# Feed-forward products from x without its root, padded chunk tiles and another order of filling, in a two-block float32 transformer kernel

## The chip, the cores and the metric

One NeuronCore of a Trainium2 chip runs the whole program in one launch. The metric is the device time in microseconds (us). Times of the kernel before are given as the median of three runs; the trace comes from one more, profiled execution.

## The reference, cut to what matters

Two transformer blocks of width D = 1024 over 256 tokens, in float32. The first block has a gated-delta-rule mixer (8 heads, chunks of 64 tokens) and one feed-forward part; the second has two layers, a gated linear attention (4 heads, chunks of 64) and a latent attention (8 heads), each with a feed-forward part. So there are three feed-forward parts, each behind a norm:

```python
def rmsnorm(t, g):                       # norm over the 1024 channels of a token
    return t * lax.rsqrt(jnp.mean(t * t, -1, keepdims=True) + EPS) * g
h = rmsnorm(x, g) * (1.0 + scale) + shift          # scale, shift: one value for a channel
gu = h @ w_ffn_in                                  # 1024 -> 2 * 2816
x = x + gate * ((silu(gu[..., :2816]) * gu[..., 2816:]) @ w_ffn_out)
# chunk step of the gated delta rule (gated linear attention has the same k_c, v form)
v_new = u_c - w_c @ state
o = q_c @ state + qk_c @ v_new
state = state * exp(gl) + k_c.T @ v_new            # k_c, v_new: 64 tokens of one chunk
```

scale, shift and gate come from products of a conditioning vector ("ada" units in the kernel).

## The kernel before, in words

All data is kept transposed: a tile has 128 channels on the partitions and the T = 256 tokens along the row; KB = 8 such tiles make x (`xT`). Each big product is made exact to float32 from fast products: a weight block of 1024 x 128 is loaded by SyncE (SP) into `w_raw` (4 slots), ScalarE copies it rounded into `w_high` (`high`, L1340 to L1345), VectorE subtracts to get `w_low` (`low`, L1845 to L1850), and the activations have the same two parts. `split_product` (L738) then issues for each of the 8 blocks k of channels three matmuls of 128x128 weights on 256 columns: high by high (L749), high by low (L750), low by high (L751); 24 matmuls make one product of 128 output channels. Everything of an engine is in one queue, and semaphores order the engines; the order of the work is written out by hand.

A feed-forward part (`ffn`, once on each engine: L753 TensorE, L1539 ScalarE, L2250 VectorE) has an up stage of 11 iterations with 4 products each (gate, up, gate, up: two pairs) and a down stage of 4 iterations with 8 pieces each. It is used for n = 1, 4 and 6. Before its first product the norm must be whole:

- VectorE adds the last output block to `xT` and squares each block into `sq` (`add_blocks`, L2156; `add_pairs`, L2202). TensorE sums the squares over partitions (`norm_sum`, L727, matmuls at L734, for blocks 6 and 7 behind the last output product).
- ScalarE makes the root: `norm` (L1319) with Ln (L1325) and Exp (L1327) gives `rstd`.
- VectorE multiplies each block by `nscale` and `rstd` (L2254), ScalarE adds shift and rounds into `h_parts` (L1549), VectorE makes the low part (`h_low`, L1861, at L1865). The first product waits for each of the 8 blocks in turn.

In the up stage ScalarE copies each product out of its PSUM bank (`bank[j % 2]`, L1337), the gates with Silu; VectorE multiplies the pair (L2273), ScalarE rounds it (L1569) and VectorE makes the low part (L2284). In iterations with an ada unit VectorE also does two multiply-adds of 512 columns for each pair (L1827).

The mixer output ahead of n = 4 and 6 comes from `out_part` (L803): plain float32 matmuls (each two records at L811) with weights in slots of `ring`, in the order of j = 0 to 7. `Stream` objects say which slots a weight stream uses: `st_o2` the slots [3, 7, 11, 16, 17, 0, 1, 2], `st_o3` the slots 4 to 11. Ring slots 0 to 3 are the memory of `w_raw`, 4 to 7 of `w_high`, 8 to 11 of `w_low`; 12 to 15 are the memory of `h1_parts`. `st_h2`, the stream of the four gated-linear-attention heads, uses splits in slots 0 to 2 only. SP issues all loads in program order, each after a wait until its slot is free.

In the delta-rule head (`head1`, L876) the step over the four chunks does `kdec[r, t, :]` by `vnew[r, t, :]` (L977) with 64 rows of partitions, r being the chunk's half of a 128-token tile; in the linear attention (`head2`, L1049) it is `kd_tok` by `v_tok` (L1094, L1104). Between such small products TensorE works off a share of the next head's split products (`products`). In the last head (`head2(H2, False, True)`) the shares are output parts instead, and the first waits for the third head's result (`head2_out`, L1066), made by VectorE at L2418.

## Time and profile before

| | us |
|---|---|
| median of three runs | 1410.51 |
| lowest and highest of them | 1408.54, 1417.34 |
| the profiled execution's own time | 1407.37 |
| its span, first to last instruction | 1405.7 |
| mean granted TensorE clock over the span | 0.978 of full speed |

The own time is 1.7 us longer than the span; what lies around the span is not touched by the change. PE is TensorE's matmuls, PEld its weight loads, DVE VectorE, ACT ScalarE, SP the queue that issues DMAs. A matmul's end is modelled in the records, so the distance from one start to the next is what to read, not its duration. A float32 matmul that is not split shows as two records.

### The profile page before, as it was taken

How to read it: one execution, taken by the hardware profiler on the slowest of the kernel's cores; microseconds unless marked ns; L12 is line 12 of the kernel's file. 1: busy time of each engine (PE TensorE's matmuls, PEld its weight loads, DVE VectorE, ACT ScalarE, POOL GpSimd, SP SyncE). 2: the span in 40 equal slices, each digit the busy share in tenths (PEclk: the TensorE clock that was granted, in tenths of full speed). 3: DMA queues.
4: the chain of work that ended last, by engine and by line, in shares of the span. 5: the costliest groups of instructions: out<-in, count | busy, mean ns of one | idle time of the engine just before them, and what ended most of it. 6: DMA issues, size and time to landing. Idle time of an engine off the chain costs nothing.

```text
span 1405.7 us, 26728 instructions
## 1 busy us (share of the span) xinstructions
PE 1324.8 (94%) x9961; PEld 1230.1 (88%) x9961; DVE 927.6 (66%) x1669; ACT 662.8 (47%) x1182; POOL 14.9 (1%) x82
## 2 busy tenths in 40 slices
PE   6899999999999899999899987999999998999997
PEld 3889899998899899999678876999997787999996
DVE  0678888788867678778655644787785542865553
ACT  2555555555555455454554423554542442545542
POOL 4000000000000000000000000000000000000000
PEclk9999999999999999999999998999999999999999
DMA  9656446555354489889668712889797383666562
GB/s 317 196 157 178 137 134 195 165 165 172 114 165 144 133 241 274 265 247 316 173 212 258 225 46 75 240 268 274 215 321 236 107 209 104 189 203 185 159 183 85
DMA packets 400017, 269.96 MB, mean 192 GB/s; under 512 B 9914, under 2 KB 357424, under 8 KB 399936
## 3 DMA queue, kind: packets, MB, share of 16 engines
q1 hardware_dynamic: 399936, 268.83, 64.2%
q8 instruction: 57, 0.93, 0.3%
q14 instruction: 24, 0.20, 0.0%
HBM read 267.75 MB, written 1.05 MB: 191 GB/s over the span
## 4 chain that ended last, share of the span: by engine, by line
PE 82%; DVE 8%; ACT 4%; issue 2%; DMA 2%; SPq 2%; DVEq 0%; ACTq 0%
PE bank L749 20%; PE bank L751 20%; PE bank L750 20%; PE bank L811 4%; DVE w_low L1849 1%; PE bank L1150 1%; PE bank L734 1%; ACT w_high L1345 1%; PE bank L941 1%; PE bank L949 1%; PE bank L950 1%; DMA ring<-in_mla_w_q_up 1%; DVE h_parts L1865 1%; SPq L534 1%; SPq L472 1%
## 5 line engine op out<-in xcount | busy, mean ns | idle before, releaser
L749 PE MATMUL bank<-h_parts,w_high 128*128 128x256 f32 x2016 | 605.0, 300 | 21.1 <-DVE h_parts L1865 16.2
L751 PE MATMUL bank<-h_parts,w_low 128*128 128x256 f32 x2016 | 576.4, 286 | 0.0
L750 PE MATMUL bank<-h_parts,w_high 128*128 128x256 f32 x1952 | 558.7, 286 | 0.0
L1849 DVE TENSOR_TENSOR w_low<-w_raw,w_high 128x1024 fp32r<-128x1024 f32 (+2 forms) x348 | 391.0, 1130 | 101.3 <-ACT w_high L1345 87.4
L749 PEld LDWEIGHTS bank<-h_parts,w_high 128*128 128x128 f32 x2016 | 391.8, 194 | 42.8 <-issue 25.3
L751 PEld LDWEIGHTS bank<-h_parts,w_low 128*128 128x128 f32 x2016 | 392.4, 195 | 0.0
L750 PEld LDWEIGHTS bank<-h_parts,w_high 128*128 128x128 f32 x1952 | 381.3, 195 | 1.3 <-issue 1.0
L1345 ACT ACTIVATE w_high<-w_raw 128x1024 fp32r<-128x1024 f32 (+2 forms) x348 | 338.1, 979 | 78.0 <-PE bank L751 28.5
L749 PE MATMUL bank<-act_parts,w_high 128*128 128x256 f32 x528 | 148.8, 282 | 0.0
L1337 ACT ACTIVATE evac<-bank 128x256 f32<-128x256 f32 x140 | 53.6, 383 | 200.5 <-PE bank L751 199.7
L750 PE MATMUL bank<-act_parts,w_high 128*128 128x256 f32 x528 | 147.4, 279 | 0.0
L751 PE MATMUL bank<-act_parts,w_low 128*128 128x256 f32 x528 | 147.4, 279 | 0.0
L749 PEld LDWEIGHTS bank<-act_parts,w_high 128*128 128x128 f32 x528 | 99.2, 188 | 1.8 <-DVE w_low L1849 1.7
L751 PEld LDWEIGHTS bank<-act_parts,w_low 128*128 128x128 f32 x528 | 99.5, 188 | 0.0
L750 PEld LDWEIGHTS bank<-act_parts,w_high 128*128 128x128 f32 x528 | 99.0, 188 | 0.1
L1827 DVE SCALAR_TENSOR_TENSOR big<-ada_w,cact,big 128x512 f32<-128x512 f32 (+1 forms) x98 | 73.3, 748 | 1.1
L811 PE MATMUL bank<-big,ring 128*128 128x256 f32 x256 | 63.1, 399 | 8.4 <-DVE big L2418 6.6
L811 PEld LDWEIGHTS bank<-big,ring 128*128 128x128 f32 x256 | 49.8, 200 | 16.5 <-DVE big L2418 7.4
L1479 ACT ACTIVATE scratch<-bank 128x256 f32<-128x256 f32 x40 | 15.4, 386 | 88.8 <-PE bank L941 88.7
L2273 DVE TENSOR_TENSOR evac<-evac 128x256 f32<-128x256 f32 x66 | 28.1, 425 | 35.1 <-ACT evac L1337 35.0
L1337 ACT ACTIVATE scratch<-bank 128x256 f32<-128x256 f32 x64 | 24.5, 383 | 54.7 <-PE bank L751 54.5
L2070 DVE TENSOR_TENSOR scratch<-scratch,bank 128x512 f32<-128x512 f32 (+1 forms) x40 | 25.4, 635 | 37.1 <-PE bank L950 37.1
(371 smaller groups left out, 1480.4 us busy)
## 6 DMA issues: line engine op xcount, KB each, us to landing
ada_w<-in_ada_w SPq DMA_DIRECT2D x48, 1024.0 KB, 6.1
w_raw<-in_ffn_w_in SPq DMA_DIRECT2D x88, 512.0 KB, 4.2
w_raw<-in_w_in SPq DMA_DIRECT2D x72, 512.0 KB, 3.8
w_raw<-in_w_ffn_in SPq DMA_DIRECT2D x44, 512.0 KB, 3.9
ada_w<-in_w_ada SPq DMA_DIRECT2D x16, 1024.0 KB, 7.3
w_raw<-in_gla_w_in SPq DMA_DIRECT2D x24, 512.0 KB, 6.2
w_raw<-in_ffn_w_out SPq DMA_DIRECT2D x32, 384.0 KB, 4.3
w_raw<-in_ffn_w_out SPq DMA_DIRECT2D x32, 320.0 KB, 3.4
```

What stands on the lines that cost most here:

```text
L472: sp.dma_start(dst, src(i, j)).then_inc(S(f"landed{s}"), 16)
L749: pe.matmul(acc[:, 0:T], hi[:, n, :], x_high[:, k, :], start=k == 0, stop=False)
L750: pe.matmul(acc[:, 0:T], hi[:, n, :], x_low[:, k, :], start=False, stop=False)
L751: mm = pe.matmul(acc[:, 0:T], lo[:, n, :], x_high[:, k, :], start=False, stop=k == kb - 1)
L811: mm = pe.matmul(accs[j // 2][:, j % 2 * T:(j % 2 + 1) * T], slot(st.slots[j])[:, k, :], rhs[:, k, :], start=k == 0 and j % 2 == 0, stop=k ...
L1337: return act.activation(dst, bank[(j % nacc)][:, 0:T], func, scale=scale).then_inc(S("evacuated"), 1)
L1345: act.activation(w_high[:, s, 0:m], w_raw[:, s, 0:m], ACT.Copy).then_inc(S("rounded"), 1)
L1479: act.activation(xs.rearrange("p a b -> p (a b)"), bank[3][:, 0:NT * P], ACT.Copy).then_inc(S("xs"), 1)
L1827: dve.scalar_tensor_tensor(acc, w, c, acc, ALU.mult, ALU.add).then_inc(S("ada_mac"), 1)
L1849: dve.tensor_tensor(w_low[:, s, 0:m], w_raw[:, s, 0:m], w_high[:, s, 0:m].bitcast(F32), ALU.subtract)\
L2070: dve.tensor_tensor(flat, flat, bank[4][:, 2 * P * part_of.start:], ALU.subtract).then_inc(S("inv"), 1)
L2273: dve.tensor_tensor(prod, prod, evac[:, 2 * q + 1, :], ALU.mult).then_inc(S("ffn_act"), 1)
```

## The change

Four things change.

1. The feed-forward parts take `xs_parts` in place of `h_parts`: x times `nscale`, without the root, in high and low parts, and as two more columns (TW = T + 2 = 258) the shift in high and low parts. Each block is made as soon as it is added: ScalarE copies it with scale (`x_high`) and also squares it, VectorE makes the low part (`x_low`), inside the loops that add the output blocks. A product thus gives W(x * nscale) in 256 columns and W(shift) in the two others. VectorE multiplies a pair's two products by `rstd_wide` (the root, and 1 in the two more columns) straight from two PSUM banks, ScalarE does Silu with column 256 as bias, VectorE adds the other's column 256 and multiplies. The first product of a part runs before its norm is whole; the last squares are summed behind it.
2. `pairs` of PSUM banks: the up stage uses banks 2, 3 and then 0, 1, the down stage 2 and 3.
3. `kdec`, `vnew` and `kd_tok` are padded with zeros, so that L977, L1094 and L1104 use all 128 rows of partitions. GpSimd clears `kdec` and `vnew` at the start; ScalarE writes 3 half tiles of `kdec` where it wrote 2 whole, and 3 of `kd_tok` where it wrote 1.
4. Filling: pieces 0 and 1 of a part's weights are split before it begins; `st_o2` uses the slots [2, 6, 10, 3, 7, 11, 16, 17] and `st_o3` [6, 7, 10, 11, 16, 17, 2, 3]; the output parts of the last linear-attention head take heads 0 and 1 for j = 0 to 5 first, then head 2.

```diff
+        TW = T + 2
+        h1_parts = x_space[:, 0:2 * KB * T].rearrange("p (k a t) -> p k a t", k=KB, a=2)
+        xs_parts = x_space.rearrange("p (k a t) -> p k a t", k=KB, a=2)
-        kdec = piece((NT, P))
+        kdec = piece((NCH, P))
-        kd_tok = piece((NT, P))
+        kd_tok = piece((NCH - 1, P))
-        st_o2 = Stream(1, KB, [3, 7, 11, 16, 17, 0, 1, 2])
+        st_o2 = Stream(1, KB, [2, 6, 10, 3, 7, 11, 16, 17])
-        st_o3 = Stream(1, KB, SplitStream.SLOTS)
+        st_o3 = Stream(1, KB, [6, 7, 10, 11, 16, 17, 2, 3])
+        HIDDEN = pairs[::-1]
+        DOWN = bank[2:4]
-            pool.memset(wz, 0.0).then_inc(S("padded"), 1)
+            for dst in (wz, kdec, vnew):
+                pool.memset(dst, 0.0).then_inc(S("padded"), 1)
...
# TensorE: split_product takes x_high.shape[-1] columns; ffn:
                     for j in range(4):
-                        pe.wait_ge(S("evacuated"), st_f.done(i, j) + 3 - 2)
-                        split_product(st_f, i, j, bank[j % 2], h_parts, ...)
+                        if j % 2 == 0:
+                            pe.wait_ge(S("evacuated"), st_f.done(i, j + 1) + 3 - 4)
+                        elif first:
+                            pe.wait_ge(S("evacuated"), st_f.block0 + 3)
+                        if first and j == 0:
+                            pe.wait_ge(S("shift_low"), m + 1)
+                        split_product(st_f, i, j, HIDDEN[j // 2][:, j % 2, :], xs_parts, ...)
+                        if first and j == 0:
+                            norm_sum(n, range(KB - 2 if n == 1 else 3, KB))
...
-                        pe.matmul(bank[4][:, 0:P], kdec[r, t, :], vnew[r, t, :], start=True, stop=True).then_inc(S("s_done"), 1)
+                        pe.matmul(bank[4][:, 0:P], kdec[:, c, :], vnew[:, t, :], start=True, stop=True).then_inc(S("s_done"), 1)
...
                             if at[0] == 0:
+                                pe.wait_ge(S("head2_out"), H2 - 2)
+                                pe.wait_ge(S("evacuated"), st_h2.end + 3)
+                            if at[0] == 6 * (KB - 2 * DV2):
                                 pe.wait_ge(S("head2_out"), H2 - 1)
-                                pe.wait_ge(S("evacuated"), st_h2.end + 3)
...
             for j in range(KB):
-                if j >= 6:
-                    norm_sum(4, range(3 * (j - 6), 3 * (j - 5)))
+                if j == 6:
+                    norm_sum(4, range(3))
                 for k in range(KB - DV2, KB):
                     out_part(st_o2, OUT2, j, k, big)
-            norm_sum(4, range(KB - 2, KB))
...
# ScalarE
+            def x_high(n, f, shift_sec):
+                act.wait_ge(S("o_added"), 4 + FFN_OF[n] * KB + f + 1)
+                if f == 0:
...
+                    act.activation(xs_parts[:, :, 0, T:TW], shift.broadcast_to([P, KB, TW - T]), ACT.Copy).then_inc(S("shift_high"), 1)
+                act.activation(xs_parts[:, f, 0, 0:T], xT[:, f, :], ACT.Copy, scale=nscale[:, f:f + 1]).then_inc(S("h_ready"), 1)
+                act.activation(sq[:, f, :], xT[:, f, :], ACT.Square).then_inc(S("norm_sq"), 1)
...
             def ffn(n, st_f, st_d, shift_sec):
-                act.wait_ge(S("gemm_done"), st_f.block0)
-                high(st_f, 0, 0, IN_PARTS)
+                high(st_f, 0, 2, IN_PARTS, free=st_f.block0)
                 norm(n)
-                for f in range(KB):
...
+                        gate = evac_wide[:, 2 * q, :]
+                        act.wait_ge(S("evacuated"), st_f.done(i, 2 * q + 1) + 3)
+                        act.activation(gate[:, 0:T], gate[:, 0:T], ACT.Silu, bias=gate[:, T:T + 1]).then_inc(S("silu"), 1)
...
# VectorE
+            def x_low(n, f, shift_sec):
+                dve.wait_ge(S("h_ready"), KB * n + f + 1)
...
+                dve.scalar_tensor_tensor(xs_parts[:, f, 1, 0:T], xT[:, f, :], nscale[:, f:f + 1], xs_parts[:, f, 0, 0:T].bitcast(F32),
+                                         ALU.mult, ALU.subtract).then_inc(S("h_low"), 1)
...
-                        dve.wait_ge(S("evacuated"), st_f.done(i, 2 * q + 1) + 3)
-                        dve.tensor_tensor(prod, prod, evac[:, 2 * q + 1, :], ALU.mult).then_inc(S("ffn_act"), 1)
+                        dve.wait_ge(S("gemm_done"), st_f.done(i, 2 * q + 1))
+                        dve.tensor_tensor(both, HIDDEN[q][:, :, 0:TW], scale, ALU.mult).then_inc(S("evacuated"), 2)
                         if not last:
                             low(st_f, i + 1, 2 * q, IN_PARTS)
...
+                        dve.wait_ge(S("silu"), 2 * H1 + first + 2 * i + q + 1)
+                        dve.scalar_tensor_tensor(prod, up[:, 0:T], up[:, T:T + 1], prod, ALU.add, ALU.mult).then_inc(S("ffn_act"), 1)
...
-                        dve.wait_ge(S("act_low"), first + 2 * i + q + 1)
-                        dve.sem_inc(S("ffn_free"), 1)
```

In the loops that add the output blocks, ScalarE has in `x_high` of block j-1 behind its copy of block j (n = 1), or of both blocks behind a pair's second copy (n = 4, 6); VectorE's square is gone and `x_low` of the block before stands there.

## Rows read from the trace of the kernel before

**Rows 1.** The page: busy us, share of the span, instructions
```profile
PE 1324.8 (94%) x9961; PEld 1230.1 (88%) x9961; DVE 927.6 (66%) x1669; ACT 662.8 (47%) x1182; POOL 14.9 (1%) x82
```
**Rows 2.** Windows; columns: stretch, length, busy PE, PEld, DVE, ACT, POOL, PEclk, DMA
```profile
161.83:204.63 42.80, 41.87 (x329) 38.89 (x328) 34.83 (x67) 22.80 (x42) 0.00 (x0) 1.00 0.55 160
...
486.00:612.00 126.00, 125.89 (x1042) 124.95 (x1043) 97.11 (x126) 63.74 (x108) 0.00 (x0) 0.99 0.88 260
```
**Rows 3.** Chain that ended last, entry of n = 1: start us, us, what
```profile
469.06 2.59 PE bank L734 x12
...
474.40 0.14 PE bank L751
...
486.11 0.55 PE bank L749
```
**Rows 4.** Timeline, ScalarE, same entry: start us, us, instruction, idle before
```profile
469.15 0.47 ACT L1337 ACTIVATE evac<-bank,mod 128x256 f32<-128x256 f32 x1 [2.40 <-PE bank L751]
474.56 1.06 ACT L1345 ACTIVATE w_high<-w_raw 128x1024 fp32r<-128x1024 f32 x1 [4.93 <-PE bank L751]
...
476.92 0.42 ACT L1327 ACTIVATE rstd<-lnb 128x256 f32<-128x256 f32 x1
477.95 0.91 ACT L1549 ACTIVATE h_parts<-hT,mod 128x256 fp32r<-128x256 f32 x2 [0.62 <-DVE hT L2254]
```
**Rows 5.** Timeline, VectorE, same entry
```profile
474.56 0.48 DVE L2164 SCALAR_TENSOR_TENSOR xT<-bank,mod,xT 128x256 f32<-128x256 f32 x1 [4.02 <-PE bank L751]
```
**Rows 6.** Timelines of ScalarE and then TensorE, entry of n = 4
```profile
857.52 0.84 ACT L1524 ACTIVATE evac<-bank,mod 128x256 f32<-128x256 f32 x2 [4.39 <-PE bank L811]
...
879.13 0.58 PE L749 MATMUL bank<-h_parts,w_high 128*128 128x256 f32 x1
```
**Rows 7.** Timeline of ScalarE and then the chain, entry of n = 6
```profile
1180.57 0.84 ACT L1524 ACTIVATE evac<-bank,mod 128x256 f32<-128x256 f32 x2 [2.15 <-PE bank L811]
...
1201.18 0.36 PE bank L749
```
**Rows 8.** Timeline, TensorE, in a delta-rule head: one chunk step
```profile
202.59 0.38 PE L970 MATMUL bank<-scratch 128*128 128x128 f32 x2
202.81 0.33 PE L973 MATMUL bank<-scratch 128*128 128x64 f32 x2
...
203.63 0.28 PE L751 MATMUL bank<-h_parts,w_low 128*128 128x256 f32 x1
203.84 0.49 PE L977 MATMUL bank<-scratch 64*128 64x128 f32 x2
204.25 0.39 PE L749 MATMUL bank<-h_parts,w_high 128*128 128x256 f32 x1
```
**Rows 9.** Timelines of TensorE and then its weight loads, a linear-attention head
```profile
766.11 1.45 PE L1094 MATMUL bank<-scratch 64*128 64x256 f32 x4
767.49 0.44 PE L1098 MATMUL bank<-scratch 128*128 128x64 f32 x2
...
768.64 0.53 PEld L1098 LDWEIGHTS bank<-scratch 128*128 128x128 f32 x4
769.09 0.19 PEld L749 LDWEIGHTS bank<-h_parts,w_high 128*128 128x128 f32 x1
```
**Rows 10.** VectorE's groups by form, 486 to 612 us; the last of 400 to 425
```profile
L1849 DVE TENSOR_TENSOR w_low<-w_raw,w_high 128x1024 fp32r<-128x1024 f32 x42 | 51.5, 1225 | 14.2 <-ACT w_high L1345 11.3
L1827 DVE SCALAR_TENSOR_TENSOR big<-ada_w,cact,big 128x512 f32<-128x512 f32 x28 | 21.0, 750 | 0.6
...
L2070 DVE TENSOR_TENSOR scratch<-scratch,bank 128x512 f32<-128x512 f32 x3 | 2.1, 690 | 4.8 <-PE bank L950 4.8
```
**Rows 11.** Page's DMA issues, SP's timeline, chain: start of the last linear-attention head
```profile
w_raw<-in_gla_w_in SPq DMA_DIRECT2D x24, 512.0 KB, 6.2
...
813.29 2.48 SPq L451 DMA_DIRECT2D ring<-in_gla_w_out  x3
...
818.04 5.41 PE bank L811 x16
```

More of the change, by code:

```diff
@@ L139, in sb @@
             return ctx.enter_context(nc.sbuf_tensor(name, shape, dt))
-        bank = [ctx.enter_context(nc.psum_tensor(f"bank{n}", [P, 512], F32)) for n in range(8)]
+        pairs = [ctx.enter_context(nc.psum_tensor(f"pair{n}", [P, 2, 512], F32)) for n in range(2)]
+        bank = [pairs[n // 2][:, n % 2, :] for n in range(4)]
+        bank += [ctx.enter_context(nc.psum_tensor(f"bank{n}", [P, 512], F32)) for n in range(4, 8)]
         ADA_BANK = bank[7]
@@ L1337, in copy_out, with high @@
                 return act.activation(dst, bank[(j % nacc)][:, 0:T], func, scale=scale).then_inc(S("evacuated"), 1)
-            def high(st, i, j, parts):
+            def high(st, i, j, parts, free=None):
                 m, s = len(parts[j % len(parts)]) * P, j % st.slots
                 act.wait_ge(S(f"landed{s}"), st.landed(i, j))
-                if st is not st_h1 or not (isinstance(i, int) and i == 0 and j < st.slots):
+                if free is not None:
+                    act.wait_ge(S("gemm_done"), free)
+                elif st is not st_h1 or not (isinstance(i, int) and i == 0 and j < st.slots):
                     act.wait_ge(S("gemm_done"), st.done(i, j) - st.slots)
@@ L1676, in head2 @@
                 act.activation(sq_o.rearrange("p d t -> p (d t)"), bank[5][:, :], ACT.Square).then_inc(S("o2_sq"), 1)
+                if not gemm:
+                    high(st_f2, 0, 0, IN_PARTS, free=st_h2.end)
                 copies(6)
@@ L1690, in _ @@
             head2(H2, False, True)
-            out_pairs(st_o2, OUT2, KB, 10)
+            high(st_f2, 0, 1, IN_PARTS, free=st_h2.end)
+            out_pairs(st_o2, OUT2, KB, 10, 4, 11)
             ffn(4, st_f2, st_d2, 11)
@@ L1795, in _ @@
             attended(st_h3.n - 1)
-            out_pairs(st_o3, OUT3, 2 * KB, 16)
+            for j in range(2):
+                high(st_f3, 0, j, IN_PARTS, free=st_d2.end)
+            out_pairs(st_o3, OUT3, 2 * KB, 16, 6, 17)
             ffn(6, st_f3, st_d3, 17)
@@ L2410, in head2 @@
                     decays(i + 1)
+                if not gemm:
+                    low(st_f2, 0, 0, IN_PARTS)
                 dve.wait_ge(S("o2_rn"), 2 * n)
@@ L2493, in _ @@
             softmax(st_h3.n - 1)
-            add_pairs(st_o3, OUT3, 4 + 2 * KB, 16)
+            norm_cols_scaled(6, *norm_cols(6))
+            for j in range(2):
+                low(st_f3, 0, j, IN_PARTS)
+            add_pairs(st_o3, OUT3, 4 + 2 * KB, 16, 6, 17)
             ffn(6, st_f3, st_d3, Units(A_FFN3, 2, 0, 0, MAC_FFN3, SUM_FFN3))
```

193 lines of the change are left out of this document (113 added, 80 removed).

## Prediction

> **What bounds the kernel now.** I read the page first: TensorE's matmuls stand for 94% of the span, its weight loads for 88%, VectorE for 66%, ScalarE for 47% [rows 1]. The reader is to see that no other engine is near full on average. Then the windows: in the up stage of n = 1, TensorE is busy for 125.89 of 126.00 us, 1042 matmuls, so one every 0.121 us, and in a delta-rule head for 41.87 of 42.80 us [rows 2]. There only what TensorE itself does, or what makes it wait, moves the end. Last the chain at the entry of each feed-forward part, which is where it leaves TensorE: 469.06, six sums of squares; 474.40, the last matmul of the output products; then nothing of the first up product but a trickle until the second product starts at 486.11 [rows 3]. The entries of n = 4 and 6 look alike [rows 6, 7]. So I look at three things: the entries, the small products in the heads, and whether VectorE, which gets more work in the up stage, stays under TensorE's pace.
>
> **Entry of n = 1.** The unit is the start of the second up product, since from there both kernels run at TensorE's pace. Before: 486.11. After: the last output product ends at 474.54 (474.40 + 0.14) [rows 3]. The first up product, 24 x 0.12 = 2.88, can follow if its blocks are there. Blocks 0 to 4 were made one output product (2.88) and more ago. Block 5: ScalarE copies block 6 out at 469.15 (0.47), then does block 5's high part and square (0.45 each by L1549's 0.91 for two) until 470.5, then splits a weight piece (1.06) until 471.6, then block 6, until 472.5 [rows 4]. VectorE adds block 7 at 474.56 + 0.48 = 475.04 [rows 5], ScalarE makes its high part by 475.6, VectorE the low part (0.48) by 476.1. TensorE wants block 7 at 474.54 + 21 x 0.12 = 477.1. So nothing stalls; weight pieces 0 and 1 are split in the loop before, which has room (ScalarE 0.47 + 0.90 + 1.06 = 2.43 in 2.88; VectorE about 0.43 + 0.48 + 1.23 = 2.14). The product ends at 477.4, the sums of blocks 6 and 7 take 2 x 0.43 (2.59 for six) [rows 3], and the second product starts at 478.3. That is 7.8 less. The first matmul at 486.11 took 0.55, not 0.12 [rows 3], because the clock had fallen in the gap; without the gap this 0.4 goes too: **8.2**.
>
> The root is no longer on TensorE's path. It comes at 478.3 + Ln + Exp (0.42 each) [rows 4] = 479.3, and VectorE needs it only when the first pair is done, at 478.3 + 2.88 = 481.2. A table load and piece 3's high part come behind it on ScalarE and its low part on VectorE, some 3.6 us in all: 482.9, wanted at 484.1. What is late next is VectorE, some 1.7 us behind its first pair, with more than 3 us until TensorE wants the banks back.
>
> **Entries of n = 4 and 6.** Here the output is made in pairs of 1.73 us (8 records of 0.216, by the twelve in 2.59) [rows 3], but ScalarE now has for a pair two copies (0.84), two high parts (0.91) and two squares (0.84): 2.6. It becomes the bound of this short stretch. From the first copy at 857.52 [rows 6] it has 7 copies x 0.42 + 8 x 0.87 = 9.9 us, with 1.2 us of handoffs to VectorE's adds; block 7's high part is there at 857.5 + 9.9 + 1.2 - 0.4 = 868.2, its low part at 868.7, and the last three matmuls end 0.36 behind it: 869.1, or somewhat later. (TensorE itself came there at 857.5 + 5.2 for three pairs + 1.3 for three sums + 0.5 of waiting for the third square = 864.5.) Five sums of squares follow (5 x 0.43 = 2.2), and the second product starts at 871.5. Before it was 879.13, the first matmul at 0.58 [rows 6]: 7.6 + 0.4 = **8.0**. For n = 6 the first copy is at 1180.57 [rows 7]; VectorE has two split pieces (2.45) just ahead, which its adds wait about 1 us for: second product at 1180.6 + 14.0 + 1.0 = 1195.5 against 1201.18, and there the clock was up (0.36): **5.7**. Raw slots 2 and 3 of n = 6 are filled only behind output parts 6 and 7, at about 1188; landing 6.2 us later (the row of a like load) [rows 11] piece 2 is split by 1196.5, wanted at 1198.4. Bounds for the three together: 26 if ScalarE's tail doesn't show (the product ends at 864.5 + 2.9 = 867.4 and not 869.1), 15 if each of some ten handoffs in a tail costs 0.3 more.
>
> **Padded tiles.** In one chunk step the full-row L970 is 0.12 behind the matmul before it and leaves after 202.81 - 202.59 = 0.22; the 64-row L977 starts 203.84 - 203.63 = 0.21 behind, and the next starts 204.25 - 203.84 = 0.41 later [rows 8]. So 64 rows cost 0.09 + 0.19 = 0.28 more. Three in each of 8 heads; the first of the three waits for VectorE anyhow, so its 0.09 stays: 8 x 0.75 = **6.0**. VectorE waits for these very products in the timeline, so it moves along. In linear attention the pair at L1094 takes 767.49 - 766.11 = 1.38 where two full ones take 0.86 [rows 9]; the second still waits for the first's end, so I take 0.35 of it, and 0.2 for the third: 4 x 0.55 = 2.2, take **2.0** as the last head hangs on other engines for a part. Bounds: 4 and 9. ScalarE's added half tiles (one in a delta-rule head, two in the other, 0.3 each) lie in front of its waits for TensorE; GpSimd's two memsets end before x has landed. If that cover were gone, it would be 8 x 0.3 + 4 x 0.6 = 4.8.
> The trace has full-row weight loads starting together with the running matmul: four in 769.09 - 768.64 = 0.45, beside others' matmuls [rows 9]. The Trainium skill (TensorE: Matmul & The Clock Gate, The mechanism) says that a weight load overlaps running matmuls only when its row group differs. By that rule padding would gain nothing, and the sum would be 21.9. The trace disagrees with it: it is the half-row load that isn't pulled ahead.
>
> **Two more columns.** 3 x 11 x 4 x 24 = 3168 matmuls go from 256 to 258 columns. In proportion to 0.121 that would be 0.9 ns each, 3.0 us. But the four weight loads in 0.45 us are 0.112 each with only 64 columns beside them, so the load alone nearly fills the 0.121 and the columns can hide behind it. I take 0; the bounds are 0 and, from the nearest dearer form of the same width, a plain float32 record of 0.216, 95 ns each or 301 us. That the 258 columns keep the cheap form I believe because they still are one instruction of one kind on one bank.
> The Trainium skill (the same page, Back-to-back issue gap) has a gap of N / 2.4 + 2.5 ns, by which two columns are 0.83 ns; as an estimate 2.6 us, and the sum 27.3.
>
> **VectorE in the up stage.** For each pair (5.8 us of TensorE) in iterations with an ada unit: two lows 2.45, two unit steps 1.50, the product with the root (516 columns out of PSUM) 0.69 by the 512-column row, Silu's partner 0.48, the low part 0.48: 5.60 [rows 5, 10]. It no longer idles for ScalarE's copies nor waits for its own low part. 5.6 < 5.8: it keeps up, barely, with a cushion of about 1.5 us behind the entry. Bounds for the new product: 0.43 to 0.96 (two of 0.48); at 0.96 the cycle is 5.87, 20 pairs x 0.07 = 1.4, within the cushion. Cost 0. ScalarE gets lighter.
>
> **Filling.** `st_o2` now starts with slots of the linear-attention stream, so all 8 loads stand behind its end at 813.29 [rows 11]. The wait for the third head's result goes, which had held TensorE until 818.04; the landing takes its place: 813.3 + 6.2 = 819.5 by the median of like loads, some 2 us less if it lands as the first on an idle queue. I take 0, bounds -0.5 and +3. The loads come at some 1.8 us each and TensorE eats them slower.
>
> **Sum.** 8.2 + 8.0 + 5.7 + 6.0 + 2.0 = 29.9. The profiled execution's 1407.4 becomes 1377.5. The median of the runs is 3.1 above it: 1410.5 - 29.9 = **1380.6**.
>
> **Rivals.**
> - The tail of ScalarE and VectorE at n = 4 and 6 eats more: the three entries give 15, not 21.9, and the last head's landing 3 the other way: 1390. For it: both engines work at their limit for ten us there. Against: each step has a row.
> - Padding gives nothing, since full-row loads wait as well in this place, or since VectorE's chain rules the heads: 1410.5 - 21.9 = 1388.6. Against: the 0.41 beside 0.22. The first half of it is the rule of the Trainium skill named above.
> - VectorE becomes the bound of the up stages. It decides from a cycle of 5.9 us; if the two-bank product took 1.5 us (no row does), the cycle is 6.4, 0.6 x 48 pairs = 29 us back: 1409.
> - Slower: 258 columns, or blocks that start at 8-byte steps, take TensorE's moving read off its cheap form. From 9.4 ns a matmul (29.9 / 3168) the gain is gone, from 14 ns it is slower by 1%; at the 95 ns of the float32 record it is 1380.6 + 301 = 1682. For it: no split matmul of another width is in the trace. Against: the weight load sets the pace.
> - The change doesn't do what it says: the first product still waits for something that comes with the root, and only the 8.0 of padding is won: 1402.5.
>
> **How the numbers follow.** Forecast 0.72 (its own range 1374 to 1388), late tails 0.12, padding nothing 0.05, VectorE the bound 0.04, wide columns 0.04, nothing at the entries 0.03. The range 1369 to 1394 takes in both first rivals and the best case (26 + 9 + 1). A measurement here tells about 1% from no change: below 1396.4 are the first three, 0.89; within 1% are VectorE as the bound and nothing at the entries, 0.06 of their 0.07; slower the wide columns and the rest, 0.05.
>
> **What would show it.** After: starts of split matmuls in the up stage still 0.120 to 0.121 apart; TensorE idle under 1 us at the entry of n = 1 and 2 to 4 at the others; L977's successor 0.2 to 0.25 behind it; VectorE some 90% busy in the up stage, with its wait for TensorE there, not the other way round. Wrong, if TensorE waits for `evac` or `w_low` inside the up stage, if the pitch is over 0.125, or if the second product of n = 4 starts more than 16 us behind the first copy.

## The result, and the profile after

The kernel after takes 1377.14 us (median of 4 runs, 1375.54 to 1380.53), against 1411.23 for the kernel before in the same session: a ratio of 0.9756, 95% interval [0.9719, 0.9793]. It is faster, by some 34 us by the medians; the two profiled executions lie 31.0 apart (own times 1407.37 and 1376.38). The prediction was 1380.6, with 29.9 for the profiled execution.

The page of the kernel after: busy us, share of the span and instructions; then groups with busy us, mean ns, idle before.
```profile
PE 1306.6 (95%) x9961; PEld 1222.8 (89%) x9961; DVE 944.5 (69%) x1692; ACT 669.3 (49%) x1159; POOL 15.6 (1%) x84
...
L2341 DVE TENSOR_TENSOR evac_wide<-pair,rstd_wide 128x516 f32<-128x516 f32 x66 | 45.8, 694 | 34.3 <-PE pair L767 34.3
```
TensorE is as full as before [rows 1], only for a shorter time. VectorE's product with the root (L2341) takes 694 ns for two banks, and it is VectorE that waits for TensorE there.

Windows of the kernel after, columns as in rows 2: the entry of n = 1, its up stage, and the entries of n = 4 and 6.
```profile
461.00:486.00 25.00, 25.00 (x200) 24.58 (x199) 17.49 (x24) 14.56 (x22) 0.00 (x0) 1.00 0.67 187
486.00:568.00 82.00, 82.00 (x693) 81.86 (x695) 73.86 (x103) 41.28 (x59) 0.00 (x0) 1.00 0.91 275
...
838.00:856.00 18.00, 17.47 (x96) 15.52 (x95) 8.32 (x18) 13.34 (x29) 0.00 (x0) 0.91 0.54 147
...
1150.00:1172.00 22.00, 19.33 (x111) 16.79 (x110) 10.59 (x20) 16.52 (x35) 0.00 (x0) 1.00 0.43 143
```
The reader is to see no idle time at all at the entry of n = 1, and VectorE at 73.86 of 82.00, 90%, in the up stage. The granted clock stands in the last column but two: 1.00, 0.91 and 1.00 at the three entries. The same windows of the kernel before, from the sums or first output parts to the second up product, have 0.84 at n = 1 (469.0 to 486.2), 0.74 at n = 4 (854.8 to 879.2) and 0.93 at n = 6 (1176.1 to 1201.2). So a part of what the entries gave is matmuls that no longer run at the lower of the two levels; how large a part stays open.

TensorE's timeline after, around the three entries: the sums of squares behind the first up product, then the first matmul of the second product. This answers to the last lines of rows 3, 6 and 7.
```profile
469.74 1.03 PE L749 MATMUL bank<-big,ones 128*128 128x256 f32 x4
470.42 0.47 PE L765 MATMUL pair<-x_space,w_high 128*128 128x258 f32 x1
...
852.45 0.47 PE L765 MATMUL pair<-x_space,w_high 128*128 128x258 f32 x1
...
1168.56 0.47 PE L765 MATMUL pair<-x_space,w_high 128*128 128x258 f32 x1
```

With such points the two executions can be laid side by side, and the 31.0 us split up by stage. "Ahead" is how much earlier the kernel after is:

| point | before | after | ahead |
|---|---|---|---|
| sums before the entry of n = 1 | 469.06 | 461.60 | 7.5 |
| second up product of n = 1 | 486.11 | 470.42 | 15.7 |
| sums behind the down stage of n = 1 | 667.54 | 652.16 | 15.4 |
| last head's output there, entry of n = 4 | 854.82 | 836.50 | 18.3 |
| second up product of n = 4 | 879.13 | 852.45 | 26.7 |
| sums behind its down stage | 1061.10 | 1034.29 | 26.8 |
| last output parts before n = 6 | 1176.15 | 1150.56 | 25.6 |
| second up product of n = 6 | 1201.18 | 1168.56 | 32.6 |
| sums behind its down stage | 1381.27 | 1349.85 | 31.4 |

So the entries gave 8.2, 8.4 and 7.0, together 23.6; the delta-rule heads 6.8 (the first split product started 0.7 earlier already); linear attention 2.9; the three feed-forward stages behind their entries lost 1.4 between them, and latent attention 1.2. Most of the 1.4 is at n = 6. There TensorE does wait once for split weights, 0.42 us at 1177.48: ScalarE had waited 3.24 us for a piece of `w_raw` to land, split it at 1175.48, and VectorE's low part of it ended at 1177.80.

Not all of the 6.8 is padding either. At 409.17 of the kernel before, in the last head, the kernel after is 5.8 ahead, 0.7 of which it had from the start. A further 1.5 come in the last 18 us of the heads, where the kernel before had a granted clock of 0.81 (409.0 to 427.3) and the kernel after 0.90 (402.0 to 418.9).

### The profile page after: what moved, and what is told of

Read it like the earlier page. It is cut to its first block, busy times and chain, and to the rows that moved or that the text cites. A ratio compares the mean times of both kernels' runs of the same rounds, so it can differ in the third digit from the quotient of the medians.

```text
span 1374.5 us, 26643 instructions
## 1 busy us (share of the span) xinstructions
PE 1306.6 (95%) x9961; PEld 1222.8 (89%) x9961; DVE 944.5 (69%) x1692; ACT 669.3 (49%) x1159; POOL 15.6 (1%) x84
## 4 chain that ended last, share of the span: by engine, by line
PE 82%; DVE 7%; ACT 3%; issue 2%; DMA 2%; SPq 2%; DVEq 0%; ACTq 0%
PE pair L765 21%; PE pair L766 20%; PE pair L767 20%; PE pair L835 3%; PE pair L1175 2%; DVE w_low L1901 1%; PE pair L965 1%; PE bank L749 1%; ACT w_high L1371 1%; PE bank L973 1%; PE bank L974 1%; DMA ring<-in_mla_w_q_up 1%; SPq L548 1%; SPq L486 1%; PE pair L1204 1%
## 5 line engine op out<-in xcount | busy, mean ns | idle before, releaser
L765 PE MATMUL pair<-x_space,w_high 128*128 128x258 f32 (+1 forms) x1888 | 558.7, 296 | 10.2 <-DVE x_space L1931 6.8
L766 PE MATMUL pair<-x_space,w_high 128*128 128x258 f32 (+1 forms) x1888 | 536.9, 284 | 0.0
L767 PE MATMUL pair<-x_space,w_low 128*128 128x258 f32 (+1 forms) x1888 | 533.1, 282 | 0.0
L765 PEld LDWEIGHTS pair<-x_space,w_high 128*128 128x128 f32 x1888 | 359.6, 190 | 25.5 <-issue 16.3
L766 PEld LDWEIGHTS pair<-x_space,w_high 128*128 128x128 f32 x1888 | 361.7, 192 | 1.6 <-issue 1.2
L767 PEld LDWEIGHTS pair<-x_space,w_low 128*128 128x128 f32 x1888 | 362.5, 192 | 0.0
L765 PE MATMUL pair<-act_parts,w_high 128*128 128x256 f32 x528 | 150.4, 285 | 0.4 <-issue 0.4
L766 PE MATMUL pair<-act_parts,w_high 128*128 128x256 f32 x528 | 149.4, 283 | 0.0
L767 PE MATMUL pair<-act_parts,w_low 128*128 128x256 f32 x528 | 149.3, 283 | 0.0
L765 PEld LDWEIGHTS pair<-act_parts,w_high 128*128 128x128 f32 x528 | 101.3, 192 | 2.3 <-issue 1.4
L766 PEld LDWEIGHTS pair<-act_parts,w_high 128*128 128x128 f32 x528 | 101.3, 192 | 0.1
L767 PEld LDWEIGHTS pair<-act_parts,w_low 128*128 128x128 f32 x528 | 101.3, 192 | 0.0
L2341 DVE TENSOR_TENSOR evac_wide<-pair,rstd_wide 128x516 f32<-128x516 f32 x66 | 45.8, 694 | 34.3 <-PE pair L767 34.3
L835 PE MATMUL pair<-big,ring 128*128 128x256 f32 x224 | 55.0, 400 | 6.6 <-DMA ring<-in_gla_w_out 3.2
```

Of the source, the lines that this page charges most:

```text
L765: pe.matmul(cols, hi[:, n, :], x_high[:, k, :], start=k == 0, stop=False)
L766: pe.matmul(cols, hi[:, n, :], x_low[:, k, :], start=False, stop=False)
L767: mm = pe.matmul(cols, lo[:, n, :], x_high[:, k, :], start=False, stop=k == kb - 1)
L835: mm = pe.matmul(accs[j // 2][:, j % 2 * T:(j % 2 + 1) * T], slot(st.slots[j])[:, k, :], rhs[:, k, :], start=k == 0 and j % 2 == 0, stop=k ...
L2341: dve.tensor_tensor(both, HIDDEN[q][:, :, 0:TW], scale, ALU.mult).then_inc(S("evacuated"), 2)
```

## The experiments

Every kernel but before_full_tiles is the one after with an edit. Own time is that of the profiled execution.

### half_tiles
```
- kdec[:, c, :], vnew[:, t, :]           + kdec[r, c, :], vnew[r, t, :]
- kd_tok[:, c, :], v_tok[:, 0, :]        + kd_tok[r, c, :], v_tok[r, 0, :]
- kd_tok[:, 2, :], v_tok[:, 1, :]        + kd_tok[0:CHUNK, 2, :], v_tok[0:CHUNK, 1, :]
```


> The kernel after, with the state products of both kinds of head reading 64 rows again (the same tiles, only the rows of the chunk), so the result is the same. Theory (a half-row weight load isn't pulled ahead of the running matmul): a delta-rule head is longer by some 0.70 us, 8 heads 5.6; a linear-attention head by some 0.5, 4 heads 2; together +7.6, so 1384.7 against 1377.1. The successor of the product at L1001 starts 0.41 behind it, not 0.2. Rival 1 (ScalarE's and VectorE's chain rules the heads): under 2 us more. Rival 2 (the heads gained by something else of the change, such as where the tiles now lie): also under 2 us, with the 0.41 there all the same.

1386.48 us, 9.3 over the kernel after by the medians; ratio to the kernel before 0.9824 [0.98, 0.9847]. TensorE's timeline and the chain, first after, then half_tiles: one chunk step, and the starts of heads four apart.
```profile
198.84 0.41 PE L1001 MATMUL bank<-scratch 128*128 128x128 f32 x2
199.09 0.39 PE L1004 MATMUL bank<-scratch 128*128 128x128 f32 x2
...
171.76 0.87 PE bank L948 x4
...
338.96 0.87 PE bank L948 x4
```
```profile
200.51 0.48 PE L1001 MATMUL bank<-scratch 64*128 64x128 f32 x2
200.93 0.49 PE L1004 MATMUL bank<-scratch 128*128 128x128 f32 x2
...
173.17 0.87 PE bank L948 x4
...
343.45 0.87 PE bank L948 x4
```
And the weight loads of that step, after and then half_tiles; the matmul in front started at 198.72 and at 200.30.
```profile
198.76 0.30 PEld L1001 LDWEIGHTS bank<-scratch 128*128 128x128 f32 x2
```
```profile
200.51 0.29 PEld L1001 LDWEIGHTS bank<-scratch 64*128 64x128 f32 x2
```
The full-row load starts 0.04 us behind the start of the matmul in front, the half-row load 0.21 behind it. The successor starts 0.42 behind the half-row product and 0.25 behind the full-row one, and four heads take 170.3 us in place of 167.2: 0.77 a head, where the prediction had 0.75. The second product of n = 1 comes 5.7 later; a linear-attention head takes 30.81 in place of 30.34, 4 x 0.47 = 1.9 more. Together 7.6, as expected. The rest of the 9.3 has no half-row product in it: in the profiled execution the 16 matmuls at L1043 took 5.18 us and not 3.63, and a weight piece landed after 9.1 us.

### before_full_tiles
The same part alone, in the kernel before: `kdec` and `kd_tok` get a tile for each chunk with the other rows zero, and the state products read all 128 rows.

> The kernel before with the full-row state products alone (both kinds of head), nothing else of the change. half_tiles gave 5.7 us in the delta-rule heads and 0.47 in each linear-attention head by the rows, 7.6 in all, but its whole time lay 9.3 above the kernel after, with a slow landing of 9.1 us and lower clocks in linear attention. If padding is worth 7.6: 1402.0 against 1409.6 of before in the same call. If what half_tiles lost beyond it belongs to padding too: 1400. If the two parts of the change hold each other up (padding is worth less with the old filling): 1404 or more. The product behind the padded one starts 0.2 us later, not 0.41.

1399.43 us, 0.9934 [0.9912, 0.9956] of the kernel before: 9.3 us less by the ratio, between 6.2 and 12.4 by its interval, more than the 7.6 of my theory, nearest to the rival's 1400. Undone or made alone, padding is worth a little over 9. The intervals are wide enough for 7.6 as well, and in the delta-rule heads the trace shows no more than the theory has: 41.4 and 42.1 us from head to head in turn, in place of 42.2 and 42.8. By the entry of n = 1 this profiled execution is 9.5 us ahead of the one of before, and the trace shows where: 1.5 come at 81 to 85 us, ahead of the first padded product, 4.9 in the heads up to 409, and 2.9 in the same hundred matmuls behind that (before, then this run):
```profile
409.00:427.30 18.30, 16.89 (x104) 15.12 (x104) 10.75 (x18) 10.94 (x14) 0.00 (x0) 0.81 0.68 214
```
```profile
402.60:417.90 15.30, 13.54 (x103) 12.43 (x103) 8.66 (x17) 10.94 (x14) 0.00 (x0) 1.00 0.81 255
```
Here, as at 81 us, the granted clock fell in before (0.81, and 0.57 at 81 to 85) and not in this run (1.00). Elsewhere it is the other way round; over the whole span both have 0.978. So what the rows tie to padding is near the 7.6, and whether the rest is padding's doing, by way of the clock, or chance stays open.

### root_first
```
+ norm_sum(n, ...)                    # ahead of the first product, not behind it
+ pe.wait_ge(S("rstd"), n + 1)
  split_product(st_f, i, 0, ...)
```


> The kernel after, but at each of the three entries the sums of squares come ahead of the first up product, and it waits for the root, though it needs no value of it. Blocks are still scaled and split without the root, while the output products run. If the gain at the entries is the root alone, nearly all of the 23.4 us that the profiles show there comes back (8.2, 8.8 and 6.2 to the end of the up stage's sum). My theory: most of it is that the eight blocks are no longer scaled and split one by one behind the root, and only the sums, ScalarE's high part, Ln and Exp and a dip of the clock come back: +3.7 at n = 1 (root some 3.9 us behind the last output product), +2.4 at n = 4 and at n = 6, where the first product had to wait for late blocks anyway; together +8.5, 1385.6.

One run, 1385.12: 8.7 more than the kernel after's own time, with 8.5 expected. The chain at the entry of n = 1 shows what the root itself costs: TensorE's last output matmul, then
```profile
468.27 0.50 DVE xT L2232
...
469.20 0.40 ACT big L1555
469.60 0.95 ACT w_high L1372
470.55 0.37 ACT lnb L1350
...
470.94 0.43 ACT rstd_wide L1352
...
471.41 0.39 PE pair L765
```
3.2 us from the last output matmul to the first of the up product. From the sums to the second product it is 2.8 longer at n = 1 and at n = 4, and 3.6 at n = 6 (14.0 in place of 10.4). Some 1.6 of these 3.6 are 17 matmuls of the first product that start 0.21 apart and not 0.12, at a granted clock that had fallen behind the wait (0.88 from 1164.4 to 1178.4, where after has 1.00 at its entry). Together it is 9.2 of the 23.6, where I expected 3.7, 2.4 and 2.4. So about three fifths of the entries' gain is not the root, but that eight blocks are no longer scaled, shifted and split one after another behind it.

### squares_shared
```
+ if n == 1 or f % 2 == 0:                       # ScalarE: even blocks only
      act.activation(sq[:, f, :], xT[:, f, :], ACT.Square)
+ if j % 2:                                      # VectorE, add_pairs
+     dve.tensor_tensor(sq[:, j, :], xT[:, j, :], xT[:, j, :], ALU.mult)
```


> The kernel after, with the squares of the odd blocks at the entries of n = 4 and n = 6 on VectorE, so that ScalarE has two copies, two high parts and one square for a pair of outputs: 2.2 us in place of 2.6, and VectorE 2.2 in place of 1.8. Theory (ScalarE is the bound of these two tails): the second up product comes 1.5 earlier at each, by at most 2.4, where TensorE's own work is the bound; together 3 less: 1373.4. Rival (the tail is a chain of handoffs between the two engines, and its length doesn't hang on ScalarE's sum): under 0.7 less. Rival (a square on VectorE stands ahead of a low part that TensorE waits for): no gain or up to 1 us more.

1377.47 us, 0.9765 [0.9737, 0.9792]: the same as after. From the sums to the second product it is 9.1 us at n = 4 (after 9.0) and 9.8 at n = 6 (after 10.4). The first rival is right. The chain after, entry of n = 4, shows why:
```profile
842.00 0.48 ACT evac_wide L1561
...
842.51 0.44 DVE xT L2283
...
842.97 0.48 DVE x_space L1924
...
843.46 0.34 DVE xT L2283
...
844.24 0.40 ACT big L1554
844.64 0.37 ACT evac_wide L1561
```
It goes to and fro: copy, add, low part, add, and only then, behind one square, the next copy. My sum of ScalarE's work (2.6 us a pair) came close to the pace, since copy to copy is 2.5 to 2.6, but it isn't the cause: a square less on ScalarE is one more on VectorE in the same ring.

### vector_extra
```
+ for e in range({1: 1, 4: 2, 6: 0}[n]):
+     dve.tensor_tensor(spare[q][e], HIDDEN[q][:, :, 0:T], root, ALU.mult)
  dve.tensor_tensor(both, HIDDEN[q][:, :, 0:TW], scale, ALU.mult).then_inc(S("evacuated"), 2)
```


> The kernel after, with VectorE's product of a pair with the root made once more into a spare tile at n = 1 (512 of its 516 columns), and twice more at n = 4; n = 6 as after. My theory of VectorE's margin: in iterations with an ada unit it is busy 5.15 of 5.72 us a pair. One product more (0.61 of its time) makes 5.76: 0 to 0.1 a pair longer over 20 pairs, 0 to 2 us at n = 1. Two more make 6.4: 0.65 a pair, 20 pairs, 13 us at n = 4, and TensorE waits there for split weights. Together 1377 to 1392, most likely 1391. Rival (the new product already takes from TensorE, by the banks or by VectorE's lag, and the split stream lives on its last slack): 12 us or more at n = 1 already. Rival (VectorE is far from the bound): under 3 us at n = 4.

One run, 1392.51. From the second product to the sums behind the down stage: n = 1 takes 181.0 us (after 181.6, so nothing lost), n = 4 193.9 against 181.8, 12.0 more: 0.60 for each of 20 pairs. (Of the other 4.1 in its own time, 2.8 are the 16 matmuls at L1043, in work that the edit doesn't touch.) VectorE's timeline, after, two successive pairs:
```profile
519.49 0.70 DVE L2341 TENSOR_TENSOR evac_wide<-pair,rstd_wide 128x516 f32<-128x516 f32 x1 [0.34 <-PE pair L767]
...
525.21 0.69 DVE L2341 TENSOR_TENSOR evac_wide<-pair,rstd_wide 128x516 f32<-128x516 f32 x1 [0.74 <-PE pair L767]
```
and in vector_extra with two more products, with a window of the same stage:
```profile
904.34 0.69 DVE L2345 TENSOR_TENSOR evac_wide<-pair,rstd_wide 128x516 f32<-128x516 f32 x1
...
910.83 0.69 DVE L2345 TENSOR_TENSOR evac_wide<-pair,rstd_wide 128x516 f32<-128x516 f32 x1
```
```profile
872.00:952.00 80.00, 77.21 (x619) 74.78 (x618) 78.60 (x116) 35.99 (x51) 0.00 (x0) 1.00 0.79 249
```
A pair goes from 5.72 us to 6.49, nothing stands idle before VectorE's product, and TensorE has fallen to 77.2 of 80. So VectorE's margin is about one such product a pair (0.6 us), and beyond it each microsecond counts.

### ring_order
```
- st_o2 = Stream(1, KB, [2, 6, 10, 3, 7, 11, 16, 17])
+ st_o2 = Stream(1, KB, [3, 7, 11, 16, 17, 2, 6, 10])
```


> The kernel after, with the eight blocks of the output weights of linear attention in ring slots 3, 7, 11, 16, 17, 2, 6, 10 instead of 2, 6, 10, 3, 7, 11, 16, 17. The first five slots aren't used by the stream before, so their loads needn't wait for its end. Theory (the filling order is where the change loses what padding wins there): TensorE's wait of 3.9 us for the landing at 796.5 goes, and with it the slower stretch behind it (16 parts in 5.23 us where the next 16 take 3.48): 5.7 less, own time 1370.7 against 1376.4. Rival 1 (the last head's chain on VectorE bounds this stretch as well): what goes there comes back as a longer wait for the last head's output, now 2.65: under 1 us less. Rival 2: slot 2 comes free late (block 5 in place of block 0), so the third weight piece of n = 4 is split late, and TensorE waits 1 to 2 us for it in the first pass: 4 less.

1373.99 us, 0.9728 [0.9704, 0.9752]: some 3 us less than after by the medians, with intervals that overlap. The chain after, then that of ring_order, at the start of linear attention (L1043) and of its last head:
```profile
682.79 3.63 PE pair L1043 x16
...
796.48 3.93 DMA ring<-in_gla_w_out
...
800.54 5.23 PE pair L835 x16
...
809.91 3.46 PE pair L835 x16
```
```profile
682.35 6.54 PE pair L1043 x16
...
799.71 3.45 PE pair L835 x16
...
807.27 3.46 PE pair L835 x16
```
The landing is gone and so is the slow first stretch behind it. From the work ahead (791.08 and 793.48) to the third group it is 18.8 us after and 13.8 here: 5.0 of the 5.7 expected. But the profiled execution lost 2.9 of it at L1043, in work that is the same in both. It stands behind a wait for the mixer's input, and how far the clock is down differs from execution to execution: 3.63 in before, after and wide, 5.0 to 6.5 in the eleven other traces. The own times lie 1.8 apart, which is 5.0 less 2.9 and 0.3 elsewhere; the medians of four runs say 3.1. The rival of the late weight piece doesn't show: from the sums to the second product of n = 4 it is 9.0 as after.

### wide
```
+ xh, xl = (x_space[:, (2 * k + a) * TW:(2 * k + a) * TW + wide] for a in range(2))   # wide: 272, 288, 320
```


> The kernel after, with more moving columns in the up products (they read on into the next part of x; the columns beyond 258 go to unused columns of the bank, so the result stays): 272 at n = 1, 288 at n = 4, 320 at n = 6, 1056 matmuls each, less the first 24. My forecast that two columns cost nothing rests on the pitch of 0.12 us being set by something other than the columns. If so, there is a width at which columns take over. Worked from the two float32 forms (0.216 us for 256 columns in four passes would be 54 ns a pass) nothing can be said of it, so: theory A (columns decide from the very first, 0.42 ns each, that is one column for each clock at 2.4 GHz, and 258 costs 0.8 ns more than 256): 125, 132 and 145 ns, +6, +13 and +27 us. Theory B (something else sets about 119, and columns take over where they need longer, at 286 columns by the same 0.42 ns): 119 to 120 at 272, 120 to 122 at 288, 133 at 320, +0, +1 and +15 us.

One run, 1426.78: 49.6 over the kernel after, where theory A has 46 and theory B 16. TensorE's timeline in the up stages of n = 1, 4 and 6, two starts each; they are 7, 8 and 7 matmuls apart.
```profile
499.89 0.29 PE L768 MATMUL pair<-x_space,w_high 128*128 128x272 f32 x1
...
500.77 0.29 PE L769 MATMUL pair<-x_space,w_high 128*128 128x272 f32 x1
...
899.81 0.29 PE L770 MATMUL pair<-x_space,w_low 128*128 128x288 f32 x1
...
900.88 0.29 PE L769 MATMUL pair<-x_space,w_high 128*128 128x288 f32 x1
...
1249.83 0.31 PE L769 MATMUL pair<-x_space,w_high 128*128 128x320 f32 x1
...
1250.86 0.31 PE L770 MATMUL pair<-x_space,w_low 128*128 128x320 f32 x1
```
Over longer stretches the starts are 126.1, 133.3 and 146.7 ns apart, with 119.2 at 258 columns: 0.50, 0.47 and 0.44 ns for each further column, from the first. From step to step it is 0.50, 0.45 and 0.42. Between 258 and 320 columns none hides behind the weight load. No run has 256 columns with x laid out as after; if the slope holds below 258 too, the two new columns cost some 0.9 ns a matmul, as an estimate 3168 x 0.9 = 2.8 us. The Trainium skill (TensorE: Matmul & The Clock Gate, Back-to-back issue gap) has N / 2.4 + 2.5 ns for a matmul by itself, 0.83 ns for two columns, and says that in a stream with weight loads both set the spacing. The trace comes to its slope at the widest step (0.42) and lies above it at the narrowest, and the constant is another: 119.2 less 258 / 2.4 leaves 11.7.

### act_at3 and all_64
Then why is the up stage no slower than before? Because something else must have made its matmuls faster, and those of the down stage slower. In the first, `act_parts` starts 64, 128 and 320 bytes further for n = 1, 4 and 6; in the second everything from the weights on does, by 64.

> In the kernel before, split matmuls that read act_parts start every 117.8 ns, in the kernel after every 120.0, and these are 1584 a run. Two things differ: act_parts starts 192 bytes further along its partition (byte 176576 before, 176768 after), and the products go to banks 2 and 3, not 0 and 1. Here act_parts starts at another byte for each feed-forward part, banks as after: 176832 at n = 1, 176896 at n = 4, 177088 (512 above where it was before) at n = 6. Theory of the place, with a period of 256 bytes (117.8 at 192 over a multiple, 118.6 at 0, 120.0 at 128, from act_parts and h_parts in the two traces): 117.8 at n = 1, 118.6 at n = 4, 117.8 at n = 6, and about 3 us less in all. With a period of 512: only n = 6 is sure to show 117.8. Theory of the bank: 120.0 in all three, and no change of the time.

> A tile of 64 bytes that nobody uses stands ahead of the ring, so that the split weights and all that they are multiplied with lie 64 bytes further, with the distance between them as after. If the pitch of split matmuls hangs on where moving data lie by themselves, it changes: 117.8 ns instead of 120.0 in the down stages (act_parts goes from 128 over a multiple of 256 to 192 over), and the heads become shorter as well, since their data too lie at 128 over one now. If it hangs on the distance between weights and data, all pitches stay: 119.2 up, 120.0 down. If it hangs on the bank, they stay too, and act_at3 tells the two apart.

act_at3 took 1372.37 (one run), 4.0 below the own time of after, where the pitch of two down stages makes 2.3; all_64 1380.69 (one run), 4.3 above it with the pitches as they were. Of these, 2.8 come ahead of the entry of n = 1, and the 16 matmuls at L1043 are 1.7 longer (5.28 us). That is how far single executions lie apart, so the place is judged by the pitch and not by these times. TensorE's timeline, down stage, two starts with 25 matmuls from the one to the other: before, after, and act_at3 at n = 1 and n = 4.
```profile
629.80 0.28 PE L749 MATMUL bank<-act_parts,w_high 128*128 128x256 f32 x1
...
632.74 0.28 PE L750 MATMUL bank<-act_parts,w_high 128*128 128x256 f32 x1
```
```profile
609.75 0.28 PE L767 MATMUL pair<-act_parts,w_low 128*128 128x256 f32 x1
...
612.75 0.28 PE L765 MATMUL pair<-act_parts,w_high 128*128 128x256 f32 x1
```
```profile
609.82 0.28 PE L771 MATMUL pair<-act_parts,w_low 128*128 128x256 f32 x1
...
612.76 0.28 PE L769 MATMUL pair<-act_parts,w_high 128*128 128x256 f32 x1
...
1009.84 0.28 PE L769 MATMUL pair<-act_parts,w_high 128*128 128x256 f32 x1
...
1012.84 0.28 PE L770 MATMUL pair<-act_parts,w_high 128*128 128x256 f32 x1
```
2.94, 3.00, 2.94 and 3.00 us: 117.8 ns in before (over longer stretches), 120.0 in after, 117.8 at n = 1 and, not shown, at n = 6, 120.0 at n = 4, with after and act_at3 in the same banks. So it isn't the bank. And all_64 keeps 120.0 down and 119.2 up: it isn't where the moving data lie by themselves either, but their distance from the weights. `w_high` starts at a multiple of 128 bytes; `act_parts` 64 bytes off such a multiple gives 117.8, on one 120.0. My guess of 118.6 for n = 4 was wrong.

### apart_64, apart_and_order, split_places
In the first `x_space`, `h_parts` and `act_parts` all start 64 bytes further, the weights stay; the second is that and ring_order.

> The kernel after, with x_space starting 64 bytes further (the split weights ahead of it stay), and h_parts and act_parts with it, so that all that is multiplied by split weights lies at a distance from them of 64 over a multiple of 128 bytes, where it was a multiple of 128. From act_at3 and all_64: split matmuls of the down stages start every 117.8 ns in place of 120.0: 1584 x 2.15 = 3.4 us. In the heads and the projections behind them (2880 split matmuls, starting every 119.3 as the mean) 117.8 as well, if it is the distance there too: 4.3 more at the best, where TensorE is the bound. The up stages keep 119.2: their rows of 1032 bytes put each block at another distance. So 1376.4 - 3.4 = 1373.0 if only the down stages answer, 1368.7 if the heads do. Rival (the place matters only for act_parts, whose pieces have six or five blocks and not eight): 1373.0, and 119.3 in the heads as before.

> apart_64 and ring_order together: the version that should beat both kernels. ring_order took the wait of 3.9 us and the slower 16 parts behind it (5.23 to 3.45), and was longer by 2.9 in the 16 matmuls at L1043, where the same wait ended in a lower clock, 6.54 in place of 3.63. If the two gains add, 1377.1 - 3.1 (ring_order's median against the one of after) - 3.4 to 7.7 = 1366.3 to 1370.6; if the first is the chance of one clock dip more or less, up to 2 us above.

apart_64: 1376.34, 0.975 [0.9722, 0.9778]; apart_and_order: 1371.46, 0.9725 [0.9704, 0.9746]. The heads and the down stages went to 117.8 as expected, but the up stages to 120.0, not kept at 119.2: 2.6 us given back. By the pitches apart_64 should then lie up to 5 us under after, and its median is 0.8 under: the time missed its forecast of 1368.7 to 1373.0. At the sums behind the down stage of n = 1 the profiled execution is still 3.5 ahead of after, at those of the next entry 0.5 behind; 2.7 of these 4.0 are L1043 again (6.37 us), the rest stays open. apart_and_order, forecast at 1366.3 to 1370.6, has the edit of ring_order on top and is 4.9 under apart_64, a second measurement of that edit. Hence the last run, with the best place for each use:
```
- h1_parts = x_space[:, 0:2 * KB * T]      + h1_parts = x_space[:, 16:16 + 2 * KB * T]
+ sb("ahead", [P, 16])                     # 64 bytes ahead of ada_w: h_parts and act_parts move
  st_o2 as in ring_order
```


> ring_order, with the parts at the place that the runs so far show to be best for each use: x of the heads (h1_parts) starts 64 bytes into x_space, h_parts and act_parts lie 64 bytes further than after, and x of the up stages (rows of 1032 bytes) stays where it was. apart_64 and apart_and_order show 117.8 ns in heads and down stages, but 120.0 in the up stages, where after has 119.2. If places work as in those runs: 117.8, 117.8 and 119.2, 3168 x 0.83 ns = 2.6 us less than apart_and_order: 1371.5 - 2.6 = 1368.9. If the up stages' pitch hangs on something else than the start of x (such as h_parts or act_parts, which moved in both runs, and don't take part in the up products), it stays 120.0 and the time 1371.5.

1368.88 us, 0.9696 [0.9671, 0.972] of the kernel before, with 117.8 ns in heads and down stages and 119.2 in the up stages. By the medians it is under both kernels, 42 us less than before and 8 less than after; against after the intervals only touch (0.9719 and 0.972).

## Why the prediction was right, point by point

- **Entry of n = 1**: 8.2 predicted, 8.2 measured; no block was late, as worked out.
- **Entries of n = 4 and 6**: 8.0 and 5.7 predicted, 8.4 and 7.0 measured. The tail from the first copy to the second product took 13.3 (839.15 to 852.45) and 13.6 us, where I had 14.0 and 15.0. The size was near, its reason was not: "it becomes the bound of this short stretch", said of ScalarE, fell with squares_shared. It is a ring of handoffs over both engines. That the sum came near is luck in part: ScalarE's 2.6 us a pair and the ring's 2.5 to 2.6 happen to agree. The extra 1.0 for VectorE's split pieces at n = 6 is the part that was mis-sized. TensorE's idle time there, forecast as 2 to 4 us, was 0.5 at n = 4 (836.5 to 852.5), where it worked at a clock of 0.89, and 2.5 at n = 6.
- **Padded tiles**: 6.0 and 2.0 predicted; 5.7 and 1.9 by the rows of half_tiles, some 9.3 by the whole times of half_tiles and before_full_tiles. It is the half-row load that isn't pulled ahead: it starts 0.21 us behind the start of the matmul in front, the full-row load 0.04. The rule of the Trainium skill (TensorE: Matmul & The Clock Gate, The mechanism), by which full-row loads shouldn't be either, would have made half_tiles equal to after; it wasn't. The same section of the Trainium skill also lets a load for the background weight buffer be pulled ahead, and the full-row loads here fit that.
- **Two more columns**: 0 predicted, and the up stages did not get slower, but the step "the load alone nearly fills the 0.121 and the columns can hide behind it" is wrong: wide shows that columns are paid from 258 on. By the slope the two cost some 2.8 us, and something else, most likely the new place of x, took more off: 120.0 to 119.2 ns in all, 2.6 us less over 3168 matmuls. That place matters for x is shown (apart_64, 120.0 at 64 bytes from it), that it makes just this difference is not. The 0 came out by luck.
- **What no term held**: `act_parts` moved by 192 bytes because tiles declared ahead of it grew, and 1584 down matmuls went from 117.8 to 120.0 ns: 3.5 us. With the 2.6 of the up stages the two leave 0.9, so the sum didn't show it.
- **VectorE in the up stage**: 0 predicted, and nothing to be seen of it at n = 1 and 4. Its cycle was put at 5.60 and is 5.1 to 5.2 (90% of 5.72), since each row's duration overlaps the next by some 0.08 us. "It decides from a cycle of 5.9" was wrong as well: it decides from TensorE's 5.72. With my own 5.60 it would have been close; with the real one there was 0.6.
- **Filling**: 0 predicted. A landing took the place of the wait for the third head, as forecast, at about the same price; ring_order shows that it cost 5.0 us that needn't have been paid. At n = 6 a weight piece came late, a later one than the piece that I had timed: the 0.42 us of waiting for split weights at 1177.48. By my own list, TensorE waiting for `w_low` inside the up stage was a sign of being wrong; it came once, and small.

The rivals "padding gives nothing", "VectorE the bound", "wide columns" and "the change doesn't do what it says" are ruled out by these runs. Late tails were the nearest miss of my own reasoning: the tails exist, but are shorter than I thought.

## What to carry to other kernels

When a value isn't needed until the result comes out of the accumulator, what is won by applying it there is mostly the elementwise chain behind it, not the value's own latency; look which engine then has to do it, and price its margin by doubling the new instruction. A sum that comes out right can hold two errors that cancel: check the pace of the bound engine stage by stage, to a tenth of a nanosecond, also in stages that the change doesn't touch. A tile that grows moves every tile declared behind it.

## What the runs showed that was not expected

- The pace of split matmuls (128x128 weights with their own load for each, 256 columns) hangs on the distance in the partition between the weights and the moving data: 117.8 ns at 64 bytes off a multiple of 128, 120.0 (119.3 in the heads, among other work) on one. For rows of 1032 bytes 119.2 at one start and 120.0 at 64 bytes from it, though the set of distances modulo 128 is the same; so the rule is not whole, and the mechanism isn't settled. The Trainium skill (TensorE: Matmul & The Clock Gate, Step-by-step: what each phase is for) says that loading the next weights takes no read bandwidth from the running matmul; here something between the two costs 2%.
- The same waits leave TensorE's clock differently from execution to execution. Ahead of the 16 matmuls at L1043 it waits twice, 3.5 us for the first split product some 8 us earlier and 1.7 to 2.1 us just before them. In after the clock was at the lower level (0.50) from 673.9 to 680.7 and up again (1.00) behind that, and they took 3.63 us; in ring_order it was at 0.50 from 681.5 to 688.3, and they took 6.54; half_tiles has 5.18. A profile of either kernel is up to 3 us off by this alone.
- In the profiled execution of after, TensorE stood still for 0.4 us at 642.4 in the down stage of n = 1 with nothing to wait for; the same stretch is 0.6 shorter in ring_order and vector_extra.
